# Two chained blocks on one core: TensorE multiplies a cleared tile 36 times ahead of its first real product

## The chip, the core and the metric

The kernel runs as one program on one core of a Trainium2 chip. The metric is the device time of one execution in microseconds (us), as the median over several executions. TensorE (PE in the profile) multiplies; VectorE (DVE), ScalarE (ACT) and GpSimd (POOL) work beside it; SyncE (SP) issues most transfers from the chip's main memory (HBM). The engines follow their own instruction streams and meet only at semaphores.

## The reference

Everything is float32, with 256 tokens of width 2048. The first block scales and shifts the normalised input by a modulation computed from a conditioning vector `c`, passes it through a pooling mixer, and adds it back. Two more layers follow (a gated delta rule and a banded attention). The change sits in the first microseconds, in this part:

```
def ada_modulation(c, w, b):
    m = jnp.dot(jax.nn.silu(c), w) + b
    shift, scale, gate = jnp.split(m, 3, axis=-1)
    return shift[:, None], scale[:, None], gate[:, None]
...
        h = rms_norm(x) * (1.0 + scale) + shift
...
def pool_mixer(h, w_in, w_grp, scale, w_out):
    u, g = jnp.split(h @ w_in, 2, axis=-1)
    ...
    pooled = jnp.stack(
        [centred_window_mean(ug[:, :, i], w) - ug[:, :, i] for i, w in enumerate(POOL_WINDOWS)],
        axis=2)
    y = jnp.einsum('btgc,gcd->btgd', pooled, w_grp).reshape(B, T, BRANCH_W) * scale
    return (y * jax.nn.silu(g)) @ w_out
```

The products `h @ w_in` are the first thing that TensorE computes. Its left half, `u`, is made in float32; all later large products split each operand into a high and a low part of a shorter format.

## The kernel before

The channels of the model lie on the 128 partitions, in 16 tiles `kt`. Five hand-written instruction streams, one for each engine, are ordered by semaphores; nothing is scheduled by a tool.

**The first stage, `u`.** For each `kt` a chain must finish before TensorE has an operand. SP brings a block of modulation weights (1 MB, `mod_ring`, L480, four slots), DVE multiplies it with `silu_b` and sums it into one column of `modv` (`mod_column`, L1595), and ACT scales the input tile with that column (`modulated`, L1182), which gives `vo[:, kt]` and raises `s_hu`. The weights of `w_in` come as two pieces of 512 KB for each `kt` (`u_ring`, L488, eight slots, four for each half). `u_part` (L742) multiplies: one call is two matmuls of 128x512, and one `kt` is eight matmuls in all. Matmuls on two float32 operands appear in the trace as two records each.

For `kt` 0 to 3 the last matmul of a tile is left out and made up later, since its PSUM bank first holds the row sums of squares (`row_sums`, L764 and L727). They free ACT to compute the reciprocal root (`s_root`). TensorE's order is: `kt` 0 to 3, `row_sums`, the first half of `kt` 4, the four left-out matmuls (each raises `s_u_used[1]`), the first half of `kt` 5, the second halves of `kt` 4 and 5, and then `kt` 6 to 15.

**Transfers.** SP issues strictly in its written order. `u_piece(kt, half)` waits for `s_u_used[half]` from `kt` 4 on, and everything written behind it waits too, modulation blocks among them. In order stand `u_piece(4, 0)`, three modulation blocks, `u_piece(5, 0)`, and then `u_piece(4, 1)`, which waits for the first of the left-out matmuls. POOL's queue brings `consts`, `window` (after `row_sums`), the gate weights (`gate_ring`, L570), and some others.

**Later stages.** From about 134 us on, slabs of weights (`raw`, L491) are split by ACT (`w_hi`, L1149) and DVE (`w_lo`, L1625) and multiplied by TensorE (L649 to L662, L717, L719). Between the slabs DVE works on the gate blocks (L1595 again, `gate_ring`). L1783 is where DVE gives back a PSUM half of the group products, after four products at L1659.

`r2` is a tile of 128x256 floats in SBUF that the first stages don't use.

Of the kernel before, what the change touches and what calls it, by code (L numbers as in the profile page):

```python
# [21 lines left out]
P = 128  # L22
D = 2048
T = 256
# [11 lines left out]
BATCH = 4  # L36
WINDOWS = (2, 4, 8, 16)
PAD = 8
REL = 2 * T + 1
MASKED = -3e38  # L40
MOD_SLOTS = 4
U_SLOTS = 8
REACH = T // 2 + PAD
PAIRS = BATCH * (T + P)
# [164 lines left out]
def program(nc, weights, mod_w, x_t, c_d, vecs_d, consts_d, window_d, w_ab_d, bias_d, out_d):  # L209
    ctx = ExitStack()  # L210
    with ctx:
        top = [nc.sbuf_base + (-nc.sbuf_base) % 64]

        def at(name, shape, dtype, offset=None):

            size = int(np.prod(shape[1:])) * 4
            if offset is None:
                offset = top[0]
                top[0] += size + (-size) % 32
            return nc.alloc_sbuf_tensor_at(name, shape, dtype, offset=offset)  # L220

        def sem(name):
            return ctx.enter_context(nc.semaphore(name))
# [28 lines left out]
        r2 = at("r2", [P, T], F32)  # L252
# [66 lines left out]
        misc = ctx.enter_context(nc.psum_tensor("misc", [P, 2048], F32))  # L319
# [140 lines left out]
        s_zb = sem("s_zb")  # L460
        s_y = sem("s_y")
        s_tail = sem("s_tail")

        block = ctx.enter_context(nc.Block())

# [81 lines left out]
        def _(pool):  # L547
# [66 lines left out]
            for j in range(4):  # L614
# [7 lines left out]
                for k, (a, b) in enumerate(((0, BATCH * T), (BATCH * T, PAIRS))):  # L622
# [4 lines left out]
            pool.dma_start(bias_x.rearrange("p (h s) -> h p s", h=HEADS),  # L627
                           bass.AP(tensor=bias_d.tensor, offset=bias_d.offset + P, ap=[[REL, HEADS], [-1, P], [1, T]])
                           ).then_inc(s_bx, 16)
# [12 lines left out]
        def _(pe):  # L642
# [96 lines left out]
            def u_part(kt, j, halves=(0, 1)):  # L739

                for half in halves:
                    last = nc.tensor.matmul(bank(2 * j + half), vo[:, kt, half * P:(half + 1) * P],  # L742
                                            u_ring[:, 2 * (kt % 4) + j // 2, j % 2 * GC:(j % 2 + 1) * GC],
                                            start=kt == 0, stop=kt == KT - 1, skip_group_check=True)
                return last

            def u_ready(kt, half):

                pe.wait_ge(s_u[2 * (kt % 4) + half], 16 * (kt // 4 + 1))

            def u_first(kt):

                pe.wait_ge(s_hu, kt + 1)
                u_ready(kt, 0)
                u_part(kt, 0)
                u_part(kt, 1).then_inc(s_u_used[0], 1)
# [11 lines left out]
            def pool_windows(j):  # L768
# [10 lines left out]
                                            window[:, j, 1], start=False, stop=m % 2 == 1, skip_group_check=True)  # L779
                last.then_inc(s_pool, 1)  # L780

            for kt in range(4):
                u_first(kt)
                u_ready(kt, 1)
                u_part(kt, 2)
                u_part(kt, 3, (1,))
# [803 lines left out]
        def _(dve):  # L1590
            own = Own(s_lo)
# [59 lines left out]
            def folded(t, done):  # L1651

                for w in (2 * T, T):
                    dve.wait_ge(*own.last())
                    add(t[:, 0:w], t[:, 0:w], t[:, w:2 * w], done=done if w == T else None)
# [58 lines left out]
            def add_squares(j):  # L1714
# [5 lines left out]
                if j == 3:  # L1720
                    folded(t0, s_sums)

            dve.wait_ge(s_vec, 16)
            nc.vector.tensor_scalar(vecs[:, V_BMOD + KT:V_BMOD + 2 * KT], vecs[:, V_BMOD + KT:V_BMOD + 2 * KT], 1.0, None,
                                    ALU.add).then_inc(own.up(s_dve), 1)
# [631 lines left out]
```

## Time and profile before

| | |
|---|---|
| device time, median of three executions | 1379.95 us (1379.42 to 1380.71) |
| span of the profiled execution | 1378.5 us, 1.45 us under the median; the profile has no other time for it |
| TensorE busy | 1359.8 us of the span |
| first TensorE matmul starts | 12.63 us into the span |
| read from HBM | 294.07 MB, 222 GB/s over the span |
| transfers in the first 120 us | about 417 GB/s |

All times of a trace count from the span's start. Durations of matmuls overlap: a matmul's record includes the time until its result is out, while the next has begun. The pace of TensorE is read from the distance between starts, and a short idle time in the waits is what a record of the one before leaves uncovered.

### The profile page before, as it was taken

What the parts mean: (1) busy time and instruction counts of PE and PEld (TensorE: products, weight loads), DVE (VectorE), ACT (ScalarE), POOL (GpSimd) and SP (SyncE); (2) the same over time, 40 slices, a digit from 0 to 9 for tenths busy, and PEclk for the clock granted to TensorE, in tenths of its full rate; (3) what the DMA queues carried; (4) which work ended last, traced back from release to release, by engine and by line L of the source; (5) the groups of instructions that cost most, each with busy time, mean ns of one, the idle gap of its engine ahead of it and who ended that gap; (6) DMA issues with size and microseconds to landing.
All of it is one profiled execution on the core that took longest, in us unless ns stands there. A gap on an engine that the chain in (4) does not pass through costs nothing.

```text
span 1378.5 us, 20389 instructions
## 1 busy us (share of the span) xinstructions
PE 1359.8 (99%) x7803; PEld 1158.3 (84%) x7803; DVE 976.6 (71%) x1262; ACT 795.3 (58%) x1024; POOL 47.2 (3%) x93
## 2 busy tenths in 40 slices
PE   6999999999999999999999999999999999999999
PEld 2446999888888888888999988888888888888887
DVE  3568989977787888799776567765656655656552
ACT  2215435465787787745788775467556566466431
POOL 0000022000000000000000000000000000000000
PEclk9999999999999999999999999999999999999999
DMA  9999899856476656464544756645555556555552
GB/s 383 408 418 379 340 383 409 299 186 210 138 265 208 192 183 221 161 237 153 193 152 141 210 186 209 204 160 186 179 183 181 172 170 208 165 175 175 176 193 83
DMA packets 79109, 305.80 MB, mean 222 GB/s; under 512 B 8928, under 2 KB 9328, under 8 KB 74544
## 3 DMA queue, kind: packets, MB, share of 16 engines
q1 hardware_dynamic: 67824, 261.30, 55.0%
q0 software_dynamic: 11200, 43.31, 8.9%
q8 instruction: 61, 1.00, 0.3%
q14 instruction: 24, 0.20, 0.0%
HBM read 294.07 MB, written 12.60 MB: 222 GB/s over the span
## 4 chain that ended last, share of the span: by engine, by line
PE 83%; DMA 9%; DVE 3%; ACT 2%; issue 1%; SPq 1%; POOL 0%; DVEq 0%; ACTq 0%; POOLq 0%
PE acc L717 42%; PE acc L719 21%; DMA gate_ring<-weights 4%; PE misc L970 3%; DMA mod_ring<-mod_w 2%; PE acc L660 2%; PE acc L661 2%; PE acc L662 2%; PE misc L742 2%; PE acc L742 2%; DMA raw<-weights 2%; PE misc L877 1%; DMA u_ring<-weights 1%; PE misc L868 1%; DVE gate_ring L1595 1%
## 5 line engine op out<-in xcount | busy, mean ns | idle before, releaser
L717 PE MATMUL acc<-b_op,w_hi 128*128 128x512 f32 x1792 | 634.4, 398 | 0.0
L1625 DVE TENSOR_TENSOR w_lo<-raw,w_hi 128x1024 fp32r<-128x1024 f32 x392 | 470.6, 1221 | 195.5 <-ACT w_hi L1149 191.3
L1149 ACT ACTIVATE w_hi<-raw 128x1024 fp32r<-128x1024 f32 x392 | 404.3, 1053 | 228.1 <-PE acc L719 119.6
L719 PE MATMUL acc<-b_op,w_lo 128*128 128x256 f32 x1792 | 499.5, 279 | 0.0
L717 PEld LDWEIGHTS acc<-b_op,w_hi 128*128 128x128 f32 x1792 | 336.3, 188 | 77.0 <-DVE vo L1669 0.2
L719 PEld LDWEIGHTS acc<-b_op,w_lo 128*128 128x128 f32 x1792 | 337.6, 188 | 0.5
L717 PE MATMUL acc<-a_op,w_hi 128*128 128x512 f32 x760 | 266.7, 396 | 0.6 <-DVEq L1805 0.6
L719 PE MATMUL acc<-a_op,w_lo 128*128 128x256 f32 x760 | 212.3, 279 | 0.0
L717 PEld LDWEIGHTS acc<-a_op,w_hi 128*128 128x128 f32 x760 | 142.6, 188 | 34.3 <-DVEq L1805 0.9
L719 PEld LDWEIGHTS acc<-a_op,w_lo 128*128 128x128 f32 x760 | 143.3, 189 | 0.1
L1595 DVE CUSTOM_DVE_ANT_0 mod_ring<-mod_ring,silu_b,vecs 128x2048 f32<-128x2048 f32 x26 | 61.1, 2349 | 46.9 <-DMA mod_ring<-mod_w 46.7
L742 PE MATMUL acc<-u_ring,vo 128*128 128x512 f32 x128 | 59.9, 613 | 13.1 <-ACT vo L1182 12.6
L742 PEld LDWEIGHTS acc<-u_ring,vo 128*128 128x128 f32 x128 | 25.1, 198 | 44.6 <-issue 31.4
L742 PE MATMUL misc<-u_ring,vo 128*128 128x512 f32 x128 | 57.5, 592 | 0.0
L660 PE MATMUL acc<-w_hi,b_op 128*128 128x512 f32 x128 | 50.2, 392 | 0.0
L661 PE MATMUL acc<-w_lo,b_op 128*128 128x512 f32 x128 | 49.9, 390 | 0.0
L662 PE MATMUL acc<-w_hi,b_op 128*128 128x512 f32 x128 | 49.8, 389 | 0.0
L1174 ACT ACTIVATE t<-acc 128x512 f32<-128x512 f32 x32 | 19.0, 594 | 53.4 <-PE acc L719 53.4
L742 PEld LDWEIGHTS misc<-u_ring,vo 128*128 128x128 f32 x128 | 24.2, 190 | 30.1 <-issue 30.1
L1182 ACT ACTIVATE vo<-xres,modv 128x256 f32<-128x256 f32 x16 | 8.1, 508 | 64.6 <-DVE modv L1595 64.6
L1900 DVE SCALAR_TENSOR_TENSOR t<-t,vecs,t 128x255 f32<-128x255 f32 (+2 forms) x96 | 38.8, 476 | 1.9 <-ACT t L1321 1.9
L1669 DVE TENSOR_TENSOR t<-acc,t 128x512 f32<-128x512 f32 x32 | 22.1, 691 | 24.5 <-ACT t L1174 23.8
(264 smaller groups left out, 1757.5 us busy)
## 6 DMA issues: line engine op xcount, KB each, us to landing
raw<-weights SPq DMA_DIRECT2D x392, 512.0 KB, 4.4
mod_ring<-mod_w SPq DMA_DIRECT2D x26, 1024.0 KB, 13.1
u_ring<-weights SPq DMA_DIRECT2D x32, 512.0 KB, 12.9
gate_ring<-weights POOLq DMA_DIRECT2D x30, 512.0 KB, 8.6
mod_late<-mod_w SPq DMA_DIRECT2D x6, 1024.0 KB, 7.6
xres<-x_t SPq DMA_DIRECT2D x4, 512.0 KB, 16.0
xres<-x_t POOLq DMA_DIRECT2D x4, 512.0 KB, 9.1
sums_b<-sums_d POOLq DMA_DIRECT2D x8, 256.0 KB, 4.7
```

Of the source, the lines that this page charges most:

```text
L660: nc.tensor.matmul(to, xh[:, t], wh, start=kt == 0, stop=False)
L661: nc.tensor.matmul(to, xh[:, t], wl, start=False, stop=False)
L662: last = nc.tensor.matmul(to, xl[:, t], wh, start=False, stop=end)
L717: nc.tensor.matmul(to, w_hi[:, slot, ch], op[:, kt], start=kt == 0, stop=False, skip_group_check=True)
L719: last = nc.tensor.matmul(to[:, 0:T], w_lo[:, slot, ch], op[:, kt, 0:T], start=False, stop=kt == KT - 1, skip_group_check=True)
L742: last = nc.tensor.matmul(bank(2 * j + half), vo[:, kt, half * P:(half + 1) * P], u_ring[:, 2 * (kt % 4) + j // 2, j % 2 * GC:(j % 2 + 1) ...
L970: last = nc.tensor.matmul(misc[:, k:k + P], tile_of(lhs, half, h), tile_of(rhs, half, h), start=True, stop=True)
L1149: nc.scalar.activation(w_hi[:, m.c % HL_SLOTS], raw[:, q.c % RAW_SLOTS], ACT.Copy).then_inc(own.up(s_hi), 1)
L1595: nc.vector.tensor_tensor_reduce(out=tile, in0=tile, in1=weight, scale=1.0, scalar=start, op0=ALU.mult, op1=ALU.add, accum_out=out).then_i ...
L1625: nc.vector.tensor_tensor(w_lo[:, slot], raw[:, q.c % RAW_SLOTS], w_hi[:, slot].bitcast(F32), ALU.subtract).then_inc(own.up(s_lo), 1)
L1669: nc.vector.tensor_tensor(out, products_of(unit_of(g) + h)[0], out, ALU.add).then_inc(own.up(s_free), 1)
L1900: ins = nc.vector.scalar_tensor_tensor(out=out, in0=src[:, m * T:(m + 1) * T - d], scalar=vecs[:, col:col + 1], in1=out, op0=ALU.mult, op1 ...
```

## The change

DVE clears `r2` as its very first instruction and raises the new semaphore `s_warm`. TensorE waits for it, and then multiplies `r2[:, 0:128]` with `r2` 36 times into columns 1536 to 1791 of `misc`, each as a product of its own. Nothing reads the result; the bank is started anew by the first real product that uses it. All else stays.

```
+WARM = 36
...
+        s_warm = sem("s_warm")
...
+            def warm():
+
+                pe.wait_ge(s_warm, 1)
+                for _ in range(WARM):
+                    nc.tensor.matmul(misc[:, 1536:1536 + T], r2[:, 0:P], r2[:], start=True, stop=True)
+
+            warm()
             for kt in range(4):
                 u_first(kt)
                 u_ready(kt, 1)
...
+            nc.vector.memset(r2[:], 0.0).then_inc(own.up(s_warm), 1)
             dve.wait_ge(s_vec, 16)
```

TensorE's stream of before begins as follows (names are tiles; one row for each run of like instructions, and the rows repeat for each `kt`).

```order
L641 UNCONDITIONAL_BRANCH
L742 MATMUL acc<-u_ring,vo 128x512 x4
L742 MATMUL misc<-u_ring,vo 128x512 x3
L742 MATMUL acc<-u_ring,vo 128x512 x4
L742 MATMUL misc<-u_ring,vo 128x512 x3
```

The same place in the changed kernel has the new row at the front (`r_64` is `r2`; line numbers have moved by two).

```order
L643 UNCONDITIONAL_BRANCH
L788 MATMUL misc<-r_64 128x256 x36
L744 MATMUL acc<-u_ring,vo 128x512 x4
L744 MATMUL misc<-u_ring,vo 128x512 x3
L744 MATMUL acc<-u_ring,vo 128x512 x4
```

All real matmuls keep their order; each now stands behind 36 others. On DVE the changed kernel begins so:

```order
L1598 UNCONDITIONAL_BRANCH
L1732 MEMSET r_64 128x256
L1734 TENSOR_SCALAR vecs<-vecs 128x16
L1604 ISA mod_ring,modv<-mod_ring,silu_b,vecs 128x2048
L1604 ISA modv 128x1
```

The memset is the only row that DVE gains.

## Rows read from the trace of the kernel before

**Rows 1.** The page: span, TensorE's busy time, the chain that ended last.

```profile
span 1378.5 us, 20389 instructions
...
PE 1359.8 (99%) x7803; PEld 1158.3 (84%) x7803; DVE 976.6 (71%) x1262; ACT 795.3 (58%) x1024; POOL 47.2 (3%) x93
...
PE 83%; DMA 9%; DVE 3%; ACT 2%; issue 1%; SPq 1%; POOL 0%; DVEq 0%; ACTq 0%; POOLq 0%
```

**Rows 2.** TensorE's timeline, 0 to 48 us: start, length in us, instructions, idle before.

```profile
12.63 6.03 PE L742 MATMUL acc<-u_ring,vo 128*128 128x512 f32 x8 [12.63 <-ACT vo L1182]
18.50 2.74 PE L742 MATMUL misc<-u_ring,vo 128*128 128x512 f32 x6
21.07 3.60 PE L742 MATMUL acc<-u_ring,vo 128*128 128x512 f32 x8
...
43.41 3.60 PE L742 MATMUL misc<-u_ring,vo 128*128 128x512 f32 x8
47.52 0.67 PE L742 MATMUL acc<-u_ring,vo 128*128 128x512 f32 x1 [0.51 <-DMA u_ring<-weights]
```

**Rows 3.** TensorE's waits over the whole span: us in total, times, longest.

```profile
PE acc L742 <- ACT vo L1182: 12.6, 1, 12.6
...
PE acc L649 <- DVEq L1783: 0.8, 1, 0.8
...
PE acc L742 <- DMA u_ring<-weights: 0.5, 1, 0.5
```

**Rows 4.** Stretch of 12 to 14 us: busy us by engine, PEclk, DMA share, GB/s.

```profile
12.00:14.00 2.00, 1.37 (x2) 0.84 (x3) 0.00 (x0) 1.45 (x2) 0.00 (x0) 1.00 1.03 428
```

**Rows 5.** TensorE's timeline at 386 us: four float32 matmuls of 128x256.

```profile
386.17 1.89 PE L877 MATMUL misc<-t,consts 128*128 128x256 f32 x8
```

**Rows 6.** Groups by line and shape, DVE: the two nearest memsets, mean ns.

```profile
L2192 DVE MEMSET p_t<- 64x256 f32 x8 | 2.2, 272 | 0.5
L1957 DVE MEMSET inv<- 128x1024 f32 x1 | 0.9, 912 | 0.3 <-DVE t L1900 0.3
```

**Rows 7.** ACT's timeline, 9 to 46 us: operands of TensorE, and the root.

```profile
19.45 0.51 ACT L1182 ACTIVATE vo<-xres,modv 128x256 f32<-128x256 f32 x1 [5.93 <-DVE modv L1595]
...
32.09 0.51 ACT L1182 ACTIVATE vo<-xres,modv 128x256 f32<-128x256 f32 x1 [4.86 <-DVE modv L1595]
...
42.03 0.42 ACT L1169 ACTIVATE roots<-roots 128x258 f32<-128x258 f32 x1
```

**Rows 8.** SP's timeline, 0 to 50 us: issues of transfers.

```profile
0.75 0.39 SPq L469 DMA_DIRECT2D c_all<-c  x1
...
32.46 14.35 SPq L488 DMA_DIRECT2D u_ring<-weights  x5
46.85 0.64 SPq L480 DMA_DIRECT2D mod_ring<-mod_w  x1
```

**Rows 9.** SP's waits, 0 to 48 us.

```profile
SPq L488 <- PE misc L742: 12.1, 2, 11.6
```

**Rows 10.** Stretches around 47 us, columns as in Rows 4.

```profile
47.00:48.00 1.00, 0.49 (x2) 0.30 (x2) 0.70 (x3) 0.51 (x1) 0.00 (x0) 1.00 0.89 340
...
50.00:60.00 10.00, 10.00 (x24) 4.37 (x23) 2.36 (x2) 0.51 (x1) 0.00 (x0) 1.00 1.02 416
```

**Rows 11.** The chain that ended last, in order of time, 32 to 48 us.

```profile
32.46 14.93 DMA u_ring<-weights
47.38 0.14 issue
47.52 3.67 PE acc L742 x8
```

**Rows 12.** The same chain, 99 to 240 us: start, us, what.

```profile
99.29 0.33 SPq L488
99.66 11.89 DMA mod_ring<-mod_w
...
115.76 13.35 DMA raw<-weights
...
174.73 9.75 DMA gate_ring<-weights
...
226.80 8.59 DMA gate_ring<-weights
...
236.83 1.67 DVE t L1659 x4
```

## Prediction

> **What bounds the kernel now.** I read the page first: TensorE is busy for 1359.8 of 1378.5 us, and the chain that ended last is TensorE for 83% and transfers for 9% [rows 1]. Then its waits: 12.6 us before the first matmul, and after that hardly any, the two of interest being 0.5 us for a weight transfer and 0.8 us for DVE at L1783 [rows 3]. So TensorE runs almost without a gap from 12.63 us to the end. Whatever delays its stream comes out at the end one for one, but for what those small waits take up. What makes it faster early is worth something only as far as no transfer stands in the way.
>
> Third, the pace in the timeline [rows 2]. From 18.50 to 21.07 us six records take 2.57 us, 0.43 us each. The first eight take 18.50 - 12.63 = 5.87 us, where eight at that pace take 3.43. They lose 2.44 us. The stretch at 12 to 14 us prints a clock of 1.00 [rows 4], so here that column does not show it and only the starts do; the loss fits a start at the lower level (1.2 instead of 2.4 GHz) of about twice 2.44, or 4.9 us, after 12 us without work.
>
> Fourth, where the 2.44 us go. Operands for kt 1 and kt 3 are ready at 19.96 and 32.60 us (start plus length in [rows 7]); TensorE takes up kt 1 only at 21.07, so it has fallen 1.1 us behind its operands. It is done with the work before the first half of kt 5 at 43.41 + 8 x 0.43, or 46.9 us, and waits 0.5 us for its weights [rows 2]. That transfer was issued at 32.46 and landed at 47.38 [rows 11], and neither its issue nor the queue ahead of it hangs on TensorE: SP issued it and then waited up to 11.6 us for TensorE before the next [rows 8, 9]. A TensorE that came 2.4 us sooner would wait 2.9 us there.
>
> **The change, part by part.**
>
> *The start.* The engines begin their own work at 0.75 us, as SP's first issue shows [rows 8]. DVE has nothing else then. The memset of 128x256 is bounded by one of 64x256 at 0.27 us and one of 128x1024 at 0.91 us [rows 6]; its columns are those of the first, so I take 0.27. With the semaphore TensorE starts at about 1.1 us. The memset itself hides under the wait for the first transfers and costs nothing.
>
> *The 36 products.* Each is a float32 matmul of 128x256, so two records. At full pace eight such records take 1.89 us with the tail of the last [rows 5]. The tail of a record is 0.16 to 0.17 us (in [rows 2], 3.60 us of length against 3.44 from 21.07 to the next start). That leaves 1.73 us for eight, 0.216 each. 72 records take 72 x 0.216 = 15.5 us. To this comes the slow beginning. The trace shows its price once, 2.44 us, and I take it again: the same half level for the same time costs the same, whatever is multiplied. The bounds are 0 (full clock at once) and 4.9 (half level for twice as long). Sum: 1.1 + 15.5 + 2.4 = 19.0 us. The idle time that was to be filled ends at 12.63.
>
> The Trainium skill ("TensorE: Matmul & The Clock Gate", Part 1) says that the number of slow matmuls at the start differs between runs of one kernel, with 6, 11 and 14 as its examples. If 6 to 14 of the half-length records were slow here, the price by that page would be 1.3 to 3.0 us instead of 2.4, an estimate, and the first real matmul would start at 17.9 to 19.6 us. The trace shows one start only, and can't say how it varies.
>
> *What is left of it at 21 us.* Before, the real stream starts at 12.63 and loses 2.44: it is as if it started at 15.07 at full pace. Now it starts at 19.0 at full pace, since TensorE has just been multiplying. TensorE is 4.0 us later than before, at every real matmul from kt 1 on. So the clock is won and more than lost. At 0.43 us for a product, about 21 products would have ended at 12.6, not 36.
>
> *What takes up part of the 4.0.* At 47 us the wait of 0.5 goes: 3.5 left. No new wait arises there. The root, ready at 42.45 us [rows 7], moves with the row sums to about 46.4, and the four made-up matmuls that need it start at 43.41 + 4.0 = 47.4.
>
> *SP and the transfers.* The second issue at L488 behind 32.46 waits for the first made-up matmul, which moves from about 44.3 to 48.3 us. Behind it stand three or four pieces of u and the modulation block of 46.85 [rows 8]. What was issued up to 32.46 is in by 47.38, so the transfer engines run dry for some 3 us, where before their rate only sinks to 340 GB/s [rows 10]. From 50 us on they are full again at 416 GB/s, so the time lost is not made good. In the u stage that hurts nobody: TensorE is 3.5 us later as well.
>
> *The second meeting, at 237 us.* Here the chain comes from transfers: from SP's wait at 99.29 over mod_ring, raw and gate_ring to DVE at 236.83, with TensorE waiting 0.8 us for it [rows 12, 3]. If this chain did not move, TensorE would keep 3.5 - 0.8 = 2.7 us. If it moves by what the transfers lost, about 3.0 us, it decides: 3.0. If it moves as far as TensorE did, 3.5 to 4.0. I take 3.0, as the gap of 3 us is the only thing that shifts full queues. After that all is TensorE's own work or its short round trips, and the lag stays.
>
> *Sum.* 1378.5 + 3.0 = 1381.5 us of span. The median stands 1.45 us above the span, so 1383.0 us, +0.22%.
>
> **Rivals.**
>
> *A, nothing is taken up.* The chain to 237 us moves with TensorE, by 4.0, or the slow start is longer. For it: SP's order ties modulation blocks to TensorE, and two waits of 0.5 and 0.8 us are all the slack. Against: queues of 12 to 15 us lie between issue and landing [rows 11, 12]. Time: 1379.95 + 4.0 to 4.9 = 1384 to 1385.
>
> *B, it ends on the other side: the filling is short enough.* If the products on the cleared tile took one pass of 0.216 us, they would end at 1.1 + 7.8 + 2.4 = 11.3 us, before 12.63, and the first real matmuls would run at full pace. The gain of 2.44 us then ends in the wait at 47 us: no change in the time, 1379.5 to 1380, with a little to gain where another run starts slower. It decides at 11.5 us of filling. Against: four like matmuls left eight records [rows 5].
>
> *C, the change doesn't do what it says.* If products of zeros didn't raise the clock, 72 records at 0.43 would end at 32.1 us, and the real stream would pay its 2.44 after that: 19.5 us late, 1398. Nothing in this trace multiplies zeros, so it can't be excluded, but the clock follows work everywhere else.
>
> *D, more is taken up.* If the slow beginning is nearly free in most runs, or the transfers don't fall behind, 1.5 to 2.5 us are left: 1381.5 to 1382.5.
>
> **How the numbers follow.** A measurement of this kernel can tell about 0.2% from no change, 2.8 us. Forecast of +3.0 (from +2.5 to +3.9): 0.58. A: 0.12. B: 0.07. C: 0.04. D: 0.16. Something outside these that makes it faster: 0.03. The forecast's own range straddles 2.8 us, and 0.45 of its 0.58 lies above. Slower by over 0.2%: 0.45 + 0.12 + 0.04 = 0.61. Faster: 0.03; even the whole 2.44 us would be 0.18%. Within: 0.36. The range leaves out B and C, part of D and the end of A: 1381.3 to 1384.8. It holds the spread of the slow start, about 0.9 us to either side, which this trace shows only once.
>
> **What would show it.** In the trace after: 72 records at the front from about 1.1 us, the first ten or so at 0.43 and the rest at 0.216; the first L744 matmul at 19 us with 0.43 from the first record on; no wait at 47 us; `u_ring`'s next issue at 48.4; a dip of the transfer share at 48 to 50 us to well under 0.9; kt 1 at 25 us. DVE's release of the PSUM half, L1783 before and L1793 now, moves from 238.5 to about 241.5 us, still with a short wait of TensorE before it. If the first real matmul stands at 12.7, the count of passes was wrong; if at 30, the clock; if the lag is 4 at 50 us and under 2 at 240, the chain of transfers had room that I don't see.

## The result, and the profile after

The changed kernel takes 1385.35 us (median of 6 executions, 1382.52 to 1386.34); the kernel before took 1379.86 us beside it. The ratio is 1.0036, with a 95% interval of 1.0025 to 1.0047: slower by 5.5 us. I had forecast slower by 3.0, with a range up to 1384.8, so the sign was right and the size too small. A second series of the same kernel (below, "again") gave 1383.76 us, ratio 1.0028 (1.0019 to 1.0037): 4.0 us slower, and inside my range of 1381.3 to 1384.8. The two intervals overlap.

The page of the changed kernel has these lines where [rows 1] stand before:

```profile
span 1383.5 us, 20534 instructions
PE 1374.5 (99%) x7875; PEld 1171.6 (85%) x7875; DVE 976.9 (71%) x1263; ACT 795.0 (57%) x1024; POOL 47.3 (3%) x93
PE 84%; DMA 6%; DVE 5%; ACT 3%; issue 1%; SPq 0%; POOL 0%; DVEq 0%; ACTq 0%; POOLq 0%
```

The span grew by 5.0 us. The profiled execution took 1385.56 us, 2.06 over its span. All later profiled executions show about 2.0 as well, so the one of before took some 1380.5 us, a little over its median. My forecast added 1.45 us for this step from span to time, half a microsecond too little. TensorE's busy time grew by 15 us, most of it in what had been idle time.

TensorE's timeline, where [rows 2] stand before:

```profile
1.20 17.29 PE L788 MATMUL misc<-r 128*128 128x256 f32 x72 [1.20 <-DVE r L1732]
18.32 3.60 PE L744 MATMUL acc<-u_ring,vo 128*128 128x512 f32 x8
21.75 2.74 PE L744 MATMUL misc<-u_ring,vo 128*128 128x512 f32 x6
24.33 3.60 PE L744 MATMUL acc<-u_ring,vo 128*128 128x512 f32 x8
```

The 36 products are 72 records and run from 1.20 to 18.32 us, 17.1 us: 15.5 at full pace and a slow start that cost 1.6 us. The first real eight take 21.75 - 18.32 = 3.43 us, full pace from the first record on. TensorE takes up kt 1 at 24.33 instead of 21.07, 3.3 us late, where I had 4.0.

TensorE's waits over the whole span, where [rows 3] stand before:

```profile
PE acc L651 <- DVEq L1793: 1.9, 1, 1.9
PE acc L719 <- DVEq L1815: 1.2, 1, 1.2
PE misc L788 <- DVE r L1732: 1.2, 1, 1.2
PE misc L979 <- ACT vo L1448: 1.0, 2, 0.5
PE misc L778 <- ACT u_tok L1211: 0.5, 1, 0.5
```

The wait for weights at 47 us is gone, as forecast. But the wait for DVE at the first PSUM half has not shrunk; it grew from 0.8 to 1.9 us. So did the next one like it, from 0.6 to 1.2 us; its row before is

```profile
PE acc L717 <- DVEq L1805: 0.6, 1, 0.6
```

TensorE's own lateness of 2.5 us at 50 to 120 us was not what it ended with. Others were later still.

The transfers, in stretches around 48 us (columns as in [rows 4], with [rows 10] before):

```profile
47.00:48.00 1.00, 1.00 (x4) 0.42 (x3) 1.00 (x1) 0.00 (x0) 0.00 (x0) 1.00 0.04 17
48.00:49.00 1.00, 1.00 (x4) 0.52 (x3) 0.83 (x3) 0.51 (x1) 0.00 (x0) 1.00 0.25 90
```

SP's timeline shows why (with [rows 8] before):

```profile
32.29 17.56 SPq L490 DMA_DIRECT2D u_ring<-weights  x5
49.90 0.49 SPq L482 DMA_DIRECT2D mod_ring<-mod_w  x1
```

The five issues at L490 now take until 49.85 us instead of 46.81, since the second of them waits for the first made-up matmul. Meanwhile everything issued before has landed, and the transfer engines stand nearly still for two microseconds: 17 and 90 GB/s, where it was 340 and 352.

The chain that ended last still comes to the meeting at 240 us from transfers and DVE (with [rows 12] before):

```profile
118.89 14.13 DMA raw<-weights
...
138.59 9.67 DMA raw<-weights
...
178.57 7.42 DMA gate_ring<-weights
...
241.53 1.67 DVE t L1668 x4
```

Its last row was at 236.83 and is at 241.53, 4.7 us late. In [rows 12] the first raw transfer took 13.35 us; the next one on the chain before was

```profile
134.68 9.23 DMA raw<-weights
```

The same two now take 14.13 and 9.67 us. That is 1.2 us of the growth. What follows doesn't keep the lag of 4.7 us: TensorE is 5.3 us late at 273 us, by the grown second wait, 6.6 at 345 us and 5.0 at the end, by the two paces that the last section shows.

### The profile page after: what moved, and what is told of

It is laid out like the page before. It is cut to its first block, busy times and chain, and to the rows that moved or that the text cites. A ratio compares the mean times of both kernels' runs of the same rounds, so it can differ in the third digit from the quotient of the medians.

```text
span 1383.5 us, 20534 instructions
## 1 busy us (share of the span) xinstructions
PE 1374.5 (99%) x7875; PEld 1171.6 (85%) x7875; DVE 976.9 (71%) x1263; ACT 795.0 (57%) x1024; POOL 47.3 (3%) x93
## 4 chain that ended last, share of the span: by engine, by line
PE 84%; DMA 6%; DVE 5%; ACT 3%; issue 1%; SPq 0%; POOL 0%; DVEq 0%; ACTq 0%; POOLq 0%
PE acc L719 41%; PE acc L721 20%; DMA raw<-weights 5%; PE misc L744 3%; PE acc L744 3%; PE misc L979 3%; PE acc L662 2%; PE acc L663 2%; PE acc L664 2%; DVE w_lo L1634 2%; PE misc L788 1%; PE misc L886 1%; PE misc L877 1%; DVE gate_ring L1604 1%; DMA mod_ring<-mod_w 1%
## 5 line engine op out<-in xcount | busy, mean ns | idle before, releaser
L719 PE MATMUL acc<-b_op,w_hi 128*128 128x512 f32 x1792 | 634.4, 398 | 0.0
L719 PEld LDWEIGHTS acc<-b_op,w_hi 128*128 128x128 f32 x1792 | 336.3, 188 | 77.0 <-issue 0.2
L719 PE MATMUL acc<-a_op,w_hi 128*128 128x512 f32 x760 | 266.3, 396 | 1.2 <-DVEq L1815 1.2
L719 PEld LDWEIGHTS acc<-a_op,w_hi 128*128 128x128 f32 x760 | 142.6, 188 | 35.3 <-DVEq L1815 1.5
```

The costliest lines, as they stand in the source:

```text
L719: nc.tensor.matmul(to, w_hi[:, slot, ch], op[:, kt], start=kt == 0, stop=False, skip_group_check=True)
```

## The experiments

A "lag" is the start of an instruction less the start of the same one in the trace before. "Time" is the median, beside the kernel before in the same series; a trace shows one execution of it, which in some series (3, 6, 7, 8, 10 and 12) took 1.3 to 2.3 us less than the median. Where nothing else is said a change is told from none by the interval of the ratio.

**1. Twenty products instead of 36.** Edit on the changed kernel:

```
-WARM = 36
+WARM = 20
```

> The changed kernel with 20 products on the cleared tile instead of 36. The trace of the changed kernel has them at 0.216 us a record and a slow start that cost 1.6 us, so they end at 1.2 + 40 x 0.216 + 1.6 = 11.4 us, before the first operand at 12.3. Theory P (the transfers: TensorE's lateness counts because SP waits for it at 44 us and the transfer engines run dry) expects the made-up matmuls some 0.5 us sooner than in the kernel before, SP's issue at about 44.0 instead of 44.47, and a time 0 to 1 us under the kernel before: 1379 to 1380. Theory Q (36 products are harmful in some other way than by being too long) expects most of the 5.5 us to stay: above 1382.

Measured: 1379.55 us against 1380.40, ratio 0.9997 (0.9988 to 1.0005). No change. The timeline of TensorE:

```profile
1.20 10.89 PE L788 MATMUL misc<-r 128*128 128x256 f32 x40 [1.20 <-DVE r L1732]
11.97 3.70 PE L744 MATMUL acc<-u_ring,vo 128*128 128x512 f32 x8
...
19.36 3.70 PE L744 MATMUL acc<-u_ring,vo 128*128 128x512 f32 x8 [1.12 <-ACT vo L1191]
```

The filling ends before the operand comes, the real matmuls run at full pace at once, and what they win is waited away: 1.1 us for the operand of kt 1, and 1.8 us for the weights at 47 us. This is rival B's mechanism, brought about by a smaller number. The 5.5 us come from the length of the filling, not from the filling itself (Q falls).

**2. Only SP late.** Edit on the kernel before, in SP's loop at kt 4:

```
                     u_piece(5, 0)
+                    sp.wait_ge(s_hu, 7)
                 u_piece(kt, 1)
```

> The kernel before, with one wait more on SP: before it issues the second half of the weights for kt 4 it waits for the seventh operand (s_hu at 7), which ACT had ready at 47.84 us. TensorE does nothing new; only this issue and all behind it move from 44.47 to about 47.9 us, by 3.4, about as in the changed kernel (47.72). Theory P (transfers) expects a gap of some 3 us in the transfers at 47 to 50 us, DVE's fill of mod_ring at 56 us to be 3.4 us late, and a time 4 to 6 us over the kernel before, 1384 to 1386, though TensorE itself starts as before. Theory R (it is TensorE's own lateness that counts, and the transfers only follow it) expects only the wait that arises for the late weights at 51 us, about 1 us: 1381.

Measured: 1383.11 us against 1380.40, ratio 1.0019 (1.0010 to 1.0028); the profiled span is 3.8 us longer. TensorE's waits and the transfers:

```profile
PE acc L743 <- ACT vo L1183: 12.3, 1, 12.3
PE misc L777 <- ACT u_tok L1203: 2.1, 1, 2.1
PE misc L971 <- ACT vo L1440: 1.0, 2, 0.5
PE acc L650 <- DVEq L1784: 0.7, 1, 0.7
```

```profile
47.00:48.00 1.00, 0.86 (x2) 0.49 (x3) 0.32 (x1) 0.46 (x1) 0.00 (x0) 1.00 0.00 0
48.00:49.00 1.00, 1.00 (x4) 0.45 (x3) 0.00 (x0) 0.00 (x0) 0.00 (x0) 1.00 0.46 102
```

TensorE starts as ever and is 0.3 us late at 60 us. The transfers stand still at 47 us and are 2.9 us late from then on. At 132 us TensorE has caught up with them and waits 2.1 us for ACT, which waits for raw slabs. Behind that wait the granted clock of TensorE falls to half:

```profile
136.20:139.50 3.30, 3.30 (x18) 3.30 (x17) 3.30 (x4) 3.30 (x5) 0.00 (x0) 0.50 0.93 328
```

It takes TensorE's lag from 2.6 us at 134.7 to 4.2 us at 139.5, and about 0.6 us of it passes into the chain, since SP's issues ahead of the next raw slab on the chain wait for these matmuls. So the gap is not all that this trace shows. Of the 11 executions, 3 have a mean clock of 0.999; the other 8 have a median of 1382.77 us, against 1380.36 for the executions of the kernel before that had 1.000. A gap in the transfers alone costs 2.4 to 2.7 us in the median. Theory R, that only TensorE's own lateness counts, expected 1 us and falls. P's 4 to 6 us were too many.

**3. One modulation block ahead of the wait.** Edit, on the changed kernel; the block is then left out of its old place:

```
                     u_piece(5, 0)
+                    mod_block(scale_at(7))
                 u_piece(kt, 1)
```

> The changed kernel with 36 products, and one transfer moved forward in SP's order: the modulation block for kt 7 (1 MB) is issued before the second half of the weights for kt 4, so that it doesn't stand behind SP's wait for TensorE. Its slot is free at 38.4 us. TensorE stays 2.5 to 3.3 us late. Theory P expects the dry stretch at 47 to 49 us to shrink by what 1 MB takes, 2.5 us, so that the transfers are only about 1 us late, and the time is set by TensorE's own 2.5 us less the wait of 0.8 it no longer has at 237 us: +1.7 to +2.5, 1381.5 to 1382.5. Theory R expects no gain from it: 1385.

Measured: 1382.76 us against 1380.40, ratio 1.0016 (1.0007 to 1.0025). TensorE is as late as in the changed kernel (real start at 18.43, lag 2.6 at 60 us), and the transfers no longer stand still:

```profile
47.00:48.00 1.00, 1.00 (x3) 0.38 (x2) 1.00 (x1) 0.00 (x0) 0.00 (x0) 1.00 1.01 411
48.00:49.00 1.00, 1.00 (x4) 0.46 (x3) 0.94 (x3) 0.43 (x1) 0.00 (x0) 1.00 0.76 183
```

They are 1.1 us late instead of 3.25, TensorE has no wait at 240 us, and its lag there is 1.7. The median is 2.4 us over the kernel before: P's +1.7 to +2.5 holds, its 1381.5 to 1382.5 us is missed by 0.3. That the 2.4 us left of 4.0 to 5.5 are TensorE's own lateness is argued and not shown: the traced execution took 1381.11 us, and in it TensorE is only 0.8 us late at 273 us. What the moved block gives back, 1.6 to 3.1 us by the medians, is not well measured either, since the interval overlaps that of "again".

**4. The same block moved in the kernel before.**

> The kernel before with the same transfer moved forward and nothing else. Theory P: the small dip in the transfers at 47 to 50 us (0.6 us) goes, and TensorE's waits for DVE at 237 and 272 us (0.8 and 0.6 us) shrink; against that, the second half of the weights for kt 4 now lands behind 1 MB more, 2.5 us later, at 51.1 us, just when TensorE wants it (51.03). 0 to 1 us under the kernel before: 1379 to 1380. Theory R: the same as before, 1380.

Measured: 1379.34 us against 1380.40, ratio 0.9991 (0.9982 to 1.0000). The transfers are 0.7 us early; TensorE is 0.1 us early at 238 and 0.4 us late at 273 us. At most 1 us, at the edge of the interval.

**5. The same late start, without products.** Edit on the kernel before, ahead of TensorE's first loop:

```
+            pe.wait_ge(s_x[1], 16)
             for kt in range(4):
```

> The kernel before, without any product on a cleared tile; TensorE waits for the second quarter of the input (landed at 18.3 us) before its first matmul. So it starts its real work at 18.3 to 18.4 us, as the changed kernel does (18.32), but after idle time. Theory P (transfers, with the clock as the trace shows it) expects the slow start of 1.6 to 2.4 us to be paid after 18.4, so TensorE is 5.0 to 5.7 us late at 21 us where the changed kernel was 3.3, SP's issue moves from 44.47 to about 49.9, the transfers are dry for about 6 us, and the time is 6 to 8 us over the kernel before, some 2 us over the changed kernel: 1386.5 to 1388. The rival S (the products on the cleared tile cost by something else than by holding TensorE, by their reads or writes) expects this kernel to be no slower than the changed one.

Measured: 1387.27 us against 1379.60, ratio 1.0052 (1.0038 to 1.0066).

```profile
17.97 5.76 PE L742 MATMUL acc<-u_ring,vo 128*128 128x512 f32 x8 [17.97 <-DMA xres<-x_t]
23.57 2.74 PE L742 MATMUL misc<-u_ring,vo 128*128 128x512 f32 x6
```

With nothing multiplied the slow start comes at 17.97 us and costs 5.60 - 3.43 = 2.2 us; TensorE's lag at 30 us is 5.1 us, against 3.25 in the changed kernel (4.8 in "again", whose real work starts 1.9 us later than here). The products on the cleared tile do raise the clock, and that is worth these 2.2 us. S falls: the late start, not the products, is what costs.

**6. Twice as many.**

> The changed kernel with 72 products instead of 36: 72 more records of 0.216 us, 15.6 us more before the first real matmul (33.9 us). Theory P: all later work of TensorE and SP's issue at 44.47 move by 18.8 us, the transfers are dry for about 18 us less what POOL and SP can still issue, and nothing takes it up: 17 to 21 us over the kernel before, 1397 to 1401. If more of it were hidden than in the changed kernel, under 1395.

Measured: 1399.68 us, ratio 1.0142 (1.0126 to 1.0157), +20 us. The first real matmul stands at 33.97 us, and transfers run at 2 GB/s from 52 to 60 us. The 15.6 us more than with 36 products come out as 14.3 to 15.9. Once the slack is used up, a microsecond at the front is a microsecond at the end.

**7. Two modulation blocks ahead of the wait,** `scale_at(7)` and `shift_at(1)`, with 36 products.

> The changed kernel with 36 products, and two modulation blocks (2 MB) issued ahead of SP's wait for TensorE at 44 us instead of one. Theory P: the dry stretch goes altogether, so that the transfers are on time and only TensorE's own 2.6 us count, less the 0.8 us it no longer waits at 237 and the 0.6 at 272 us: a span 0.5 to 1.7 us over the kernel before's, 1380.5 to 1382. Theory R (the transfers don't matter): as the changed kernel, 1385. Against P also speaks that the weights for kt 4 now stand behind 2 MB; they would land near 53 us, where TensorE wants them at 53.5.

Measured: 1382.98 us, ratio 1.0019 (1.0010 to 1.0028); +3.4, outside my 0.5 to 1.7. The transfers are now 0.8 us early until 120 us, and it is no better than one block. From 130 us on DVE is 1.4 us late all the same: there it waits for what TensorE, 3.0 us late, makes. That is in one trace, of an execution 1.9 us under the median; where the rest of the 3.4 us comes from stays open.

**8. Twenty products and one block moved.**

> 20 products on the cleared tile and one modulation block moved ahead of SP's wait. Theory P: both edits take something off the start of the transfers, but TensorE's waits for weights at 47 and 51 us grow by what it comes sooner, and behind 50 us only the waits of 0.8 and 0.6 us at 237 and 272 us are left to win. 0.5 to 1.5 us under the kernel before, 1378.5 to 1379.5; about as either edit alone.

Measured: 1380.54 us against 1379.60, ratio 1.0003 (0.9994 to 1.0012): no change, and not the 0.5 to 1.5 us forecast. The wait at 47 us grew to 2.4 us.

**9 and 10. POOL's first gate blocks later.** By byte count the transfers are 3.25 us late from 51 to 123 us, but DVE is 4.35 us late at 145 and 4.7 at 238 us. I took the first gate block for the cause, which moved less than the raw slabs. Edit on POOL, in the changed kernel (9) and in the kernel before (10):

```
                         pool.wait_ge(s_u_sum, 1)
+                        pool.wait_ge(s_lo, 4)
```

> The changed kernel with 36 products, and POOL's first gate block (512 KB, issued at 119.2 us) waiting until the first four raw slabs are split (s_lo at 4, about 135 us). It is needed at 154.7 us. Theory G: the transfers are 3.25 us late from 51 to 123 us, but the first raw slab lands 3.9 us late, because the gate block is released by TensorE (2.5 us late) and so enters the queues closer behind the raw slabs (3.1 us late) than before, and takes room from them. Then the slab lands about 0.6 us sooner or more, and the chain at 237 us is 3.3 to 4.0 us late instead of 4.7: a time 0.5 to 1.5 us under the changed kernel. Theory H: the extra lateness comes from something else in the stretch of 125 to 180 us: no change against the changed kernel.

> The same wait on POOL in the kernel before. By theory G the raw slabs land sooner here too, by up to 1.2 us (what 512 KB take), TensorE's waits of 0.8 us at 237 us and 0.6 at 272 us go, and the time falls by 0 to 1.2 us. Theory H: no change.

Measured: 1388.10 us with 36 products (ratio 1.0059, 1.0046 to 1.0073) and 1383.30 us without (1.0020, 1.0010 to 1.0029), both slower. The first half of the theory held: in 10 the first raw slab landed at 122.6 instead of 124.1 us. But the two gate blocks then met the next slab that the chain hangs on. In the trace before it took 9.2 us; the chain of waits in 10 and in 9 has it as

```profile
134.52 11.43 DMA raw<-weights
```

```profile
137.84 12.71 DMA raw<-weights
```

The remedy falls. The chain does show a step that sets the time in this stretch: DVE's lag at 145 us, where it takes up that slab, is within 0.7 us of TensorE's at 238 us in every trace of the table below.

The medians of 9 and 10 hold a second cost, the clock. In 9 TensorE waits 4.1 us for DVE at 241 us, and its granted clock falls to half:

```profile
PE acc L652 <- DVEq L1794: 4.1, 1, 4.1
```

```profile
244.80:248.10 3.30, 2.90 (x13) 2.90 (x14) 3.15 (x4) 2.64 (x3) 0.00 (x0) 0.50 1.04 413
```

Its lag goes from 6.6 us at the end of that wait to 7.9 us. All 5 executions of 9 have a mean clock under 1.000, and none of the 17 of the changed kernel has. In 10 it is 7 of 11 executions: they took 1383.24 to 1384.56 us, the other 4 only 1379.97 to 1381.55 us. So of the 3.5 us of 10 about 1.3 are there at full clock. The traced execution is one of those 4, with a wait of 2.9 us at the same place and no fall, so no trace shows where the others lost their clock.

**11. The changed kernel again.**

> The changed kernel as it is, a second time, on the chip of its neighbours here, to have another trace of it. If the steps found in its first trace are the rule, TensorE is again 2.3 to 3.3 us late at 50 us and 4.2 to 5.2 us late at 240 us, and the time is 4 to 6 us over the kernel before. If the growth between 50 and 240 us was chance, the lag stays near 3.

Measured: 1383.76 us against 1379.79, ratio 1.0028 (1.0019 to 1.0037). In its trace the filling runs to 19.84 us, with a slow start of 3.1 us instead of 1.6; the transfers are 5.1 us late, and here the lag does not grow after that: 5.0 at 145 and at 238 us.

```profile
1.20 18.80 PE L788 MATMUL misc<-r 128*128 128x256 f32 x72 [1.20 <-DVE r L1732]
19.84 3.60 PE L744 MATMUL acc<-u_ring,vo 128*128 128x512 f32 x8
```

**12. Twenty products and late gate blocks.**

> 20 products and POOL's first gate block behind the fourth split slab. By theory G the best that these edits give together: TensorE's waits at 237 and 272 us go. 1 to 2 us under the kernel before, at the edge of what can be told. By theory H as 20 products alone, 0 to 1 us under it.

Measured: 1382.62 us, ratio 1.0019 (1.0010 to 1.0028): as slow as 10, and G's best case falls with it. Here 6 of 11 executions have a mean clock under 1.000; the other 5 have a median of 1381.47 us, 1.7 us over the kernel before at full clock.

The lags side by side, worked out from the traces (us; the transfers' lag is that of the 35th megabyte moved, the last column is the span less 1378.5):

```
run                 first   slow   TensorE  transfers  DVE    TensorE  span
                    real    start  at 60    at 88      at 145 at 238
36 products         18.32   1.6     2.5      3.25       4.35   4.7      5.0
36, again           19.84   3.1     4.0      5.1        5.0    5.0      3.0
20                  11.97   2.1     0.4     -0.9       -1.1   -0.6     -1.2
SP late             12.28   2.3     0.3      2.9        3.7    4.1      3.8
36, one block       18.43   1.7     2.6      1.1        1.4    1.7      0.6
none, one block     12.32   1.85    0.0     -0.7       -0.7   -0.1     -0.9
20, one block       12.26   2.4     1.15    -0.8        0.1    0.2     -1.3
36, two blocks      18.66   1.9     3.0     -0.8        1.4    2.05     0.6
late, no products   17.97   2.2     4.3      4.85       6.4    6.7      6.5
72                  33.97   1.7    18.15    19.4       19.8   19.6     17.7
gate late, 36       19.11   2.4     3.3      4.1        6.6    6.6      7.2
gate late, none     12.49   2.4     0.0     -0.25       2.0    2.1      1.0
gate late, 20       12.71   2.9     0.5     -1.0        0.6    0.3     -0.2
```

## Why the prediction was too small

**What bounds the kernel: right.** TensorE has nowhere to catch up.

**The start and the 36 products: right.** 1.20 us against 1.1, 15.5 us at full pace, two records each. The first real matmul was expected at 19.0 and came at 18.32 and 19.84 in the two traces. The difference is the slow start, 1.6 and 3.1 us for my 2.4. So TensorE was 3.3 and 4.8 us late at kt 1, where I had 4.0.

**What they win: right.** 2.44 us at the front were worth nothing, as experiment 1 shows: with the clock won and no lateness, the time is the same.

**What takes up part of it: right at 47 us.** The wait for weights is gone, and TensorE went on 2.5 us late (4.0 in "again"), where I had 3.5.

**SP and the transfers: the mechanism was right, the size a little small.** The issue went to 47.72 us (I had 48.3), the gap is there, and nothing makes it good before 123 us. The lag was 3.25 us where I had 3.0, and 5.1 us in the execution with the longer slow start. Experiment 2 shows that it is a cause of its own: a gap alone costs 2.4 to 2.7 us. Without most of the gap the change costs 2.4 instead of 4.0 to 5.5 (experiment 3), but without any of it 3.4 (experiment 7), so the medians don't settle whether the gap or TensorE's own lateness is the larger part.

**The second meeting, at 237 us: here the prediction failed.** "If it moves by what the transfers lost, about 3.0 us, it decides: 3.0." It decided, but it moved by 4.7. I let the lag pass unchanged through 110 us of transfers from two queues, DVE and ACT. The chain was 3.1 us late at 115 us, as the transfers were, and 4.35 us late at 145 us: its two raw transfers took 1.2 us longer than before (14.13 and 9.67 us against 13.35 and 9.23). The rest, about 0.4 us, came by 238 us. It also grew in "late, no products" (4.85 to 6.7) and in "SP late" (2.9 to 4.1, where some 0.6 us are the fallen clock), and not in "again" (5.1 to 5.0). In this stretch raw, mod_late and gate blocks share the transfer engines and each is released by another engine. Experiments 9, 10 and 12 show that a shift of the first gate blocks against the slabs moves DVE by 1.7 to 2.3 us at 145 us, each against the same kernel without the shift. Which block is in whose way in the changed kernel is not settled; my guess, the first gate block, was wrong as a remedy.

"After that all is TensorE's own work or its short round trips, and the lag stays" failed too: the second wait for DVE added 0.6 us by 273 us, and the slow pace of the last section moved the lag up and down by more than 1 us. "Again" ends at 3.0 us of span, my number, but by luck: its lag is 5.0 us at 238 us, and the pace takes 1.3 us of it back, and a wait that it no longer has at 272 us another 0.7.

**Rivals.** A said that the chain moves with TensorE, by 4.0, or the slow start is longer, 1384 to 1385. That is nearer to what happened in the first series, but not by its mechanism: TensorE itself was 2.5 us late at 60 us, and the chain moved by more than TensorE. In "again" its second half is what the trace shows, a longer slow start of 3.1 us. B holds for 20 products. C falls: 72 records took 17.1 us, so zeros do raise the clock. D is not seen: the transfers were 3.25 and 5.1 us late.

## What to carry to other kernels

Filling idle time on an engine is safe only if it ends before the first real operand; count records, not calls, and add the slow start, which varies. Here 20 products fit and 36 didn't, and even those that fit won nothing, because the next thing waited for was a transfer. When an engine is made late, look for the queue that waits for it: a stall of an in-order issuing queue empties full transfer engines, and that lateness can be larger than the engine's own (3.25 against 2.5 us here). Whether a transfer that doesn't need the late engine gains by standing ahead of the wait is less sure: with 36 products and with none the medians were lower, but hardly clear of the noise, and with 20 it was no lower. And when a change lengthens a wait of TensorE, compare the mean granted clock of every execution, as a single trace can miss that it fell.

## What the hardware showed that I had not expected

The slow start differs between executions of like kernels: it cost 1.6 to 3.1 us in the traces above. In the two traces of the changed kernel, 7 and 14 of the 72 records start over 0.35 us before the next, and nearly all others 0.216 us. The Trainium skill ("TensorE: Matmul & The Clock Gate", Part 1) calls it run-variable; the traces agree.

The clock also fell in the middle of a kernel, after a wait of 2.1 us (experiment 2) and one of 4.1 us (experiment 9), and cost TensorE 1.6 and 1.3 us of lag; after one of 2.9 us (the trace of experiment 10) it did not.

TensorE has two paces in the large stages at the same granted clock of 1.00. A pair of records at L717 and L719 starts every 347 ns in some stretches and every 353 ns in others. The views below are of the kernel before and of the changed kernel, at like work. The first number in brackets is the count of matmuls in 20 us, which shows the difference only as 117 against 116; the distances of starts and the lag show it better.

```profile
300.00:320.00 20.00, 20.00 (x117) 17.64 (x116) 15.27 (x19) 10.64 (x14) 0.00 (x0) 1.00 0.58 189
840.00:860.00 20.00, 20.00 (x116) 17.34 (x115) 15.55 (x21) 9.86 (x13) 0.00 (x0) 1.00 0.61 194
```

```profile
300.00:320.00 20.00, 20.00 (x116) 17.32 (x115) 15.74 (x22) 11.35 (x17) 0.00 (x0) 1.00 0.56 188
845.00:865.00 20.00, 20.00 (x117) 17.51 (x116) 16.27 (x22) 9.76 (x12) 0.00 (x0) 1.00 0.62 207
```

The trace before has the slow pace from about 810 to 890 us, where the changed kernel's lag falls from 6.4 to 4.9 us; the changed kernel's has it from about 275 to 345 us, where its lag grows from 5.3 to 6.6 us. Each such stretch is worth 1.1 to 1.5 us, and it is why a span need not follow the lag at 238 us: in "again" the lag is 5.0 us there and 3.0 at the end, the 0.7 us that TensorE no longer waits at 272 us included. It could be part of the spread of 1377.7 to 1383.2 us in 35 executions of the kernel before, which no trace of them shows; the slowest of these has a mean clock of 0.998, so the clock is another part. What sets the pace no run here tells.
